# Changing the seam between two layers of a fused decoder step: the last six output strips of the first block computed by token halves, with its norms, residual and the first key and value strips

## The reference

```
layer 0:  proj = rms_norm(x, g_pre0) @ a_w_in                  # 2048 -> 2 x 2560
          xr, gate = halves of proj;  xc = causal conv(xr), 4 taps
          h = gated linear recurrence over the tokens (RG-LRU)
          out = (h * silu(gate)) @ a_w_out                     # 2560 -> 2048
          x1 = x + rms_norm(out, g_post0)
shared:   s = rms_norm(x1, kv_norm);  k = s @ w_k;  v = s @ w_v   # 4 heads of 128
layer 1:  q, gate = rms_norm(x1, g_pre1) @ b_w_in              # 16 heads of 128
          o = stick_breaking_attention(q, k, v, paged cache);  out = (o * silu(gate)) @ b_w_out
          y = x1 + rms_norm(out, g_post1)
outputs:  y, the new k and v, the last conv inputs (3 rows) and the last h of every sequence
rms_norm(x, g) = x / sqrt(mean(x*x over the width) + 1e-6) * g
```

## Time and profile before

| | us |
|---|---|
| median of 3 runs | 1816.08 (1814.78 to 1818.33) |
| profiled execution, its own time | 1814.62 |
| its span in the trace | 1812.9 |
| PE busy | 1740.7 (96%) |
| PE weight loads busy | 1666.8 (92%) |
| DVE busy | 1041.8 (57%) |
| ACT busy | 846.8 (47%) |
| POOL busy | 232.2 (13%) |
| share of PE in the chain that ended last | 88% |

### The profile page before, as it was taken

The page is one execution under the profiler, slowest core; times in us unless marked ns, Lnnn a source line. Parts: engine busy times, 40 slices in busy tenths (PEclk is TensorE's granted clock), DMA queues, the critical chain, the costliest instruction groups (busy, mean ns, idle before and its releaser), DMA issues.

```text
span 1812.9 us, 35653 instructions
## 1 busy us (share of the span) xinstructions
PE 1740.7 (96%) x14127; PEld 1666.8 (92%) x14127; DVE 1041.8 (57%) x1725; ACT 846.8 (47%) x1310; POOL 232.2 (13%) x175
## 2 busy tenths in 40 slices
PE   6999999999999999996999999999999999999997
PEld 5999999999999999995899999999998888799995
DVE  4766556666557522227757566565665666632365
ACT  4444443344444322223366666665675555722343
POOL 2000000000000000102132222322421111001110
PEclk9999999999999999998999999999999999999997
DMA  8322323322322223325432222222224777623565
GB/s 250 109 84 80 92 81 91 94 83 79 92 81 70 82 87 87 87 87 165 134 94 59 67 74 70 72 71 59 83 59 133 216 231 217 183 71 92 140 182 178
DMA packets 293525, 197.98 MB, mean 109 GB/s; under 512 B 8379, under 2 KB 267579, under 8 KB 293307
## 3 DMA queue, kind: packets, MB, share of 16 engines
q1 hardware_dynamic: 290632, 187.36, 35.4%
q0 software_dynamic: 2720, 8.78, 1.3%
q10 hardware_dynamic: 68, 0.41, 0.1%
HBM read 180.55 MB, written 15.97 MB: 108 GB/s over the span
## 4 chain that ended last, share of the span: by engine, by line
PE 88%; DVE 7%; issue 2%; ACT 1%; DMA 1%; SPq 0%; POOL 0%; ACTq 0%; DVEq 0%
PE PS L727 25%; PE PS L729 24%; PE PS L728 24%; PE Z L996 2%; PE Z L1006 1%; PE Z L727 1%; PE Z L729 1%; PE Z L728 1%; DVE T L1960 1%; DMA xin<-in_x_prompt_dram 1%; DVE WS L1672 1%; PE Z L1030 1%; PE Z L1189 1%; PE Z L905 1%; PE Z L936 1%
## 5 line engine op out<-in xcount | busy, mean ns | idle before, releaser
L727 PE MATMUL PS<-U,WS 128*128 128x272 f32 x3680 | 1075.7, 292 | 26.8 <-DVE U L1937 14.6
L729 PE MATMUL PS<-U,WS 128*128 128x272 f32 x3680 | 1065.2, 289 | 0.0
L728 PE MATMUL PS<-U,WS 128*128 128x272 f32 x3680 | 1062.6, 289 | 0.0
L727 PEld LDWEIGHTS PS<-U,WS 128*128 128x128 f32 x3680 | 694.5, 189 | 40.9 <-issue 25.1
L728 PEld LDWEIGHTS PS<-U,WS 128*128 128x128 f32 x3680 | 694.2, 189 | 0.9
L729 PEld LDWEIGHTS PS<-U,WS 128*128 128x128 f32 x3680 | 693.7, 188 | 0.0
L1672 DVE TENSOR_TENSOR WS<-raw,WS 128x1024 fp32r<-128x1024 f32 (+1 forms) x223 | 278.5, 1249 | 372.9 <-ACT WS L1221 369.9
L1221 ACT ACTIVATE WS<-raw 128x1024 fp32r<-128x1024 f32 (+1 forms) x225 | 231.1, 1027 | 531.2 <-PE PS L729 529.4
L640 POOL TENSOR_TENSOR raw<-raw,GN 128x1024 f32<-128x1024 f32 x80 | 157.9, 1974 | 556.3 <-DMA raw<-in_b_w_in_dram 470.5
L649 POOL COPY T<-T 128x544 f32<-128x544 f32 x2 | 1.7, 866 | 609.2 <-ACT T L1360 560.9
L652 POOL TENSOR_TENSOR T<-T 128x544 f32<-128x544 f32 x24 | 34.2, 1427 | 280.4 <-ACT T L1360 280.4
(11 more groups left out here) (288 smaller groups left out, 2042.2 us busy)
## 6 DMA issues: line engine op xcount, KB each, us to landing
raw<-in_a_w_in_dram SPq DMA_DIRECT2D x80, 512.0 KB, 3.8
raw<-in_b_w_in_dram SPq DMA_DIRECT2D x64, 512.0 KB, 4.1
raw<-in_a_w_out_dram SPq DMA_DIRECT2D x32, 512.0 KB, 3.9
KPG<-in_cache_k_dram SPq DMA_DIRECT2D x64, 256.0 KB, 3.2
raw<-in_b_w_out_dram SPq DMA_DIRECT2D x32, 512.0 KB, 4.0
VPG<-in_cache_v_dram SPq DMA_DIRECT2D x60, 256.0 KB, 3.0
RAW<-in_b_w_out_dram SPq DMA_DIRECT2D x12, 512.0 KB, 4.5
scratch_x<-T POOLq DMA_DIRECT2D x16, 272.0 KB, 3.6
```

The costliest lines, as they stand in the source:

```text
L727: pe.matmul(psum, w_hi, x_hi, start=first, stop=False)
L728: pe.matmul(psum, w_hi, x_lo, start=False, stop=False)
L729: return pe.matmul(psum, w_lo, x_hi, start=False, stop=last)
```

## The change

The last six strips of B are computed by token halves, in the way of E's last six: first the six strips for tokens 0 to 271 (units v = 0 to 17), then for tokens 272 to 543 (v = 18 to 35). A half strip is 20 tiles x 3 = 60 matmuls, in units of 8, 8 and 4 tiles. The first norm is done for each half by itself (3 columns of sums, the root on 128 x 3 values, then spread by a diagonal matrix). While PE works on the units from v = 21 on, the residual of the first half is done, one tile behind each unit, with its high part, square and rest; PE adds its squares from unit 23 on. The units of the first k and v strips are loaded as units 36 to 39 of the same ring, and both strips run for the first half and then, tile by tile, for the second. ACT takes them out of PSUM unscaled; DVE scales them after the second norm. The turns of k and v go to D's unit 6. The state rows are turned within B's second pair, one group behind each unit, and POOL stores them.

```diff
-D0 = B0 + 3 * KD
+B_FULL, B_SPLIT = KD - 6, 6
+BH0 = B0 + 3 * B_FULL
+BH_UNITS = 6 * B_SPLIT
+X1_AT = 3 * B_SPLIT + 3
+D0 = BH0 + BH_UNITS
+RING2 = (BH_UNITS + 4) // 4
...
-TURN_AT = {4: 0, **{FIRST_STEP - 1 + 2 * HEAD_STRIPS * k: k for k in range(1, NKV)}}
+TURN_AT = {FIRST_STEP - 1 + 2 * HEAD_STRIPS * k: k for k in range(NKV)}
...
+            def load_half_b(v):
+                if v < 2:
+                    sp.wait_ge(w_low, BH0 + v - 1)
+                elif v < 4:
+                    sp.wait_ge(state_out, 64)
                 else:
-                    col = (k * GRP + g) * DH + (D if kind == "gate" else 0)
-                    src = w_in_b[:, u * UT:(u + 1) * UT, col:col + DH]
-                load_unit(D0 + n, u, src)
-            for n in range(2):
-                load_d(n)
+                    sp.wait_ge(w_low, BH0 + v - 3)
+                if v < BH_UNITS:
+                    o, u = b_strip(v)[1], v % 3
+                    from_ = w_out_a[:, u * UT:u * UT + B_TILES[u], o * P:(o + 1) * P]
+                else:
+                    from_ = d_weights(v - BH_UNITS)
+                sp.dma_start(half_raw(v)[:, 0:b_tiles(v)], from_).then_inc((unit_in, b_half_in)[v // 2 % 2][v % 2], 16)
             sp.wait_ge(y_done, KR)
             for o in range(4):
-                reload(xT, False, o)
-            for n in range(2, 4):
+                for h in range(2):
+                    reload(h, o)
+            for v in range(BH_UNITS + 4):
+                load_half_b(v)
+                for o in range(4, KD):
+                    if min(X1_AT + o + 3, BH_UNITS + 3) == v:
+                        reload(0, o)
...
-                sp.wait_ge(x1_sum, o + 1)
+                sp.wait_ge(x1_sum[0], o + 1)
+                sp.wait_ge(x1_sum[1], o + 1)
                 sp.dma_start(x1T[o], Y[:, o, :]).then_inc(x1_kept, 16)
                 if o + 4 < KD:
-                    reload(xT, False, o + 4)
-            sp.wait_ge(st_out, 5)
-            conv_p, h_p, conv_s, h_s = out[2], out[3], out[6], out[7]
-            sp.dma_start(conv_p[0, 0], srow[ST_CP:ST_CP + SW, :]).then_inc(stored, 16)
-            sp.dma_start(h_p[0], srow[ST_HP:ST_HP + 1, :]).then_inc(stored, 16)
-            sp.dma_start(conv_s.rearrange("b l w n -> (b l w) n"), srow[ST_CS:ST_CS + NB * SW, :]).then_inc(stored, 16)
-            sp.dma_start(h_s.rearrange("b l n -> (b l) n"), srow[ST_HS:SCOLS, :]).then_inc(stored, 16)
+                    reload(1, o + 4)
...
+            for hs in range(2 * B_SPLIT - 1):
+                add_half_square(hs)
+            for n in range(3):
+                fold_first(n)
+            add_half_square(2 * B_SPLIT - 1)
+            fold_first(3)
...
+            def turn_states(n):
+                pe.wait_ge(gates_out, 4 * NBLK)
+                pe.wait_ge(y_done, KR)
                 if n >= 2:
                     pe.wait_ge(st_out, n - 1)
                 for t in range(4):
                     ins = pe.transpose(Z[0:SCOLS, 1, n % 2, t * P:(t + 1) * P], SO[:, 4 * n + t, :], IDN[:])
                 ins.then_inc(st_t, 1)
...
+            pair_b(1, lambda n: turn_states(n) if n < 5 else None)
...
+            def first_sums(h):
+                if h == 0:
+                    pe.wait_ge(st_out, 5)
+                pe.wait_ge(sq_sum, B_FULL + B_SPLIT * (h + 1))
+                for t, c in enumerate(HALF_COLS):
+                    ins = pe.matmul(Z[:, 1, 0, t:t + 1], T[:, 6, h * HALF + c:h * HALF + c + P], ONE[:, 0:1],
+                                    start=True, stop=True)
+                ins.then_inc(ms_done, 1)
+            def first_spread(h):
+                pe.wait_ge(diag_ready, 2 + h)
+                pe.matmul(Z[:, 1, 1, 0:HALF], ONE[:], T[:, 7, half(h)], start=True, stop=True).then_inc(ms_done, 1)
+            def square_sum(h, o):
+                pe.wait_ge(x1_sq[h], o + 1)
+                pe.matmul(Z[:, 0, h, 0:HALF], ONE[:], T[:, 4 + o % 2, half(h)], start=o == 0, stop=o == KD - 1,
+                          skip_group_check=True).then_inc(x1_squares[h], 1)
...
+            for v in range(BH_UNITS):
+                half_unit_b(v)
+                if v == 3 * B_SPLIT:
+                    first_sums(0)
+                if v == 3 * B_SPLIT + 1:
+                    first_spread(0)
+                if v >= X1_AT + 2:
+                    square_sum(0, v - X1_AT - 2)
+            def first_head(h, kt, s):
+                parts = half_parts(BH_UNITS + 2 * s + kt // UT)
+                c = kt % UT
+                pe.wait_ge(x1_low[h], kt + 1)
+                return three_pass(PS[:, s, h, 0:HALF], parts[:, 0, c, :], parts[:, 1, c, :], U[:, x_hi(kt), half(h)],
+                                  U[:, x_lo(kt), half(h)], kt == 0, kt == KD - 1)
+            pe.wait_ge(w_low, D0 + 1)
+            for kt in range(UT):
+                first_head(0, kt, 0)
+            square_sum(0, BH_UNITS - X1_AT - 2)
+            first_sums(1)
+            pe.wait_ge(w_low, D0 + 3)
+            for kt in range(UT):
+                first_head(0, kt, 1)
+            first_spread(1)
+            pe.wait_ge(w_low, D0 + 4)
+            for kt in range(UT, KD):
+                for s in range(2):
+                    ins = first_head(0, kt, s)
+                    if kt == KD - 1:
+                        ins.then_inc(kv_half, 1)
+                if kt > BH_UNITS - X1_AT - 2:
+                    square_sum(0, kt)
+            for kt in range(KD):
+                for s in range(2):
+                    if kt == 0:
+                        pe.wait_ge(strip_out, SD0 - 1 + s)
+                    ins = first_head(1, kt, s)
+                    if kt % UT == UT - 1:
+                        ins.then_inc(unit_done, 1)
+                if kt:
+                    square_sum(1, kt - 1)
+            square_sum(1, KD - 1)
...
+            def half_high_b(v):
+                if v < 2:
+                    act.wait_ge(unit_done, BH0 + v - 1)
+                elif v >= 4:
+                    act.wait_ge(unit_done, BH0 + v - 3)
+                if v >= BH_UNITS:
+                    act.wait_ge(w_fold, v - BH_UNITS + 1)
+                elif v // 2 % 2:
+                    act.wait_ge(b_half_in[v % 2], 16 * (v // 4 + 1))
+                else:
+                    act.wait_ge(unit_in[v % 2], 16 * (BH0 // 2 + v // 4 + 1))
+                nc.scalar.activation(half_parts(v)[:, 0, 0:b_tiles(v)], half_raw(v)[:, 0:b_tiles(v)], ACT.Copy).then_inc(w_high, 1)
...
+            def x1_split(h, o):
+                act.wait_ge(x1_sum[h], o + 1)
+                nc.scalar.activation(U[:, o, half(h)], Y[:, o, half(h)], ACT.Copy).then_inc(x1_high[h], 1)
+                if o >= 2:
+                    act.wait_ge(x1_squares[h], o - 1)
+                elif o == 0:
+                    act.wait_ge(sq_sum, B_FULL + B_SPLIT * (h + 1))
+                nc.scalar.activation(T[:, 4 + o % 2, half(h)], Y[:, o, half(h)], ACT.Square).then_inc(x1_sq[h], 1)
+            half_high_b(1)
+            for v in range(BH_UNITS):
+                half_high_b(v + 2)
+                if v and v % 3 == 0:
+                    half_square_b(v // 3 - 1)
+                if v == 3 * B_SPLIT + 1:
+                    first_root(0)
+                if v >= X1_AT:
+                    x1_split(0, v - X1_AT)
+            half_high_b(BH_UNITS + 2)
+            half_square_b(2 * B_SPLIT - 1)
+            for o in range(BH_UNITS - X1_AT, KD):
+                x1_split(0, o)
+            first_root(1)
+            half_high_b(BH_UNITS + 3)
             for o in range(KD):
-                act.wait_ge(x1_sum, o + 1)
-                nc.scalar.activation(U[:, o, :], Y[:, o, :], ACT.Copy).then_inc(x1_high, 1)
-                square(KD + o, o % 2, Y[:, o, :])
-                if o == UT + 2:
-                    high(D0 + 2, 0, 0, folded=True)
-            root(2)
+                x1_split(1, o)
+                if o == UT + 3:
+                    for which in range(2):
+                        act.wait_ge(kv_half, which + 1)
+                        act.wait_ge(ms_done, 2 + which)
+                        nc.scalar.activation(T[:, 6 + which, half(0)], PS[:, which, 0, 0:HALF], ACT.Copy)
+                    high(D0 + 4, 0, 0, done=D0 + 1, folded=True)
+            for which in range(2):
+                act.wait_ge(unit_done, D0 + 3 + which)
+                act.wait_ge(ms_done, 4 + which)
+                nc.scalar.activation(T[:, 6 + which, half(1)], PS[:, which, 1, 0:HALF], ACT.Copy).then_inc(strip_out, 1)
+            high(D0 + 5, 1, 0, done=D0 + 3, folded=True)
+            root2()
...
+            def first_norm(h):
+                hms, hy, hr, ht = (RT[:, n, 0:3] for n in range(4))
+                dve.wait_ge(ms_done, 2 + 2 * h)
+                V.tensor_scalar(hms, Z[:, 1, 0, 0:3], 1.0 / D, EPS, ALU.mult, ALU.add).then_inc(ms_out, 1)
+                dve.wait_ge(ms_root, 2 + h)
+                steps.done(V.reciprocal(hr, hy))
```

(74 more changed lines are left out.)

243 lines of the change are left out of this document (142 added, 101 removed).

## The result

The changed kernel takes 1821.56 us (median of 15 runs) where the kernel before takes 1817.21 in the same comparison: ratio 1.0023, 95% interval 1.0016 to 1.0030. It is slower by 0.23%, or 4.3 us. The forecast was 5.1 us slower, at 1821.2.

What follows compares the result with a forecast made beforehand. PE was taken as full except in one hole, where 25.2 us could be won; the new order's losses summed to 30.3, so 5.1 us longer, 1821.2 us, range 1811 to 1828.

Steps and rivals of the forecast that it cites:

- Transposes: The 20 state transposes, moved between units of B's second pair: the same 2.4 us of PE, nothing to add.
- Start of the halves: Turn from full to half strips in B: PE loses 1.3 us (0.5 to 2), as at E's identical turn.
- Tail and folds: First half, units 21 to 35: ACT and DVE alternate, +5.9 us; POOL folding gain into units 36 to 39, +2.8.
- Norm of the second half: First k tile to second half's norm: a chain of 10.5 us where PE has 3.5 of work, +7.0 (3 to 9).
- Behind the small sums: After PE's sums for the second half's norm: fourth fold holds DVE, +2.2 us; 8 tiles at lower clock, +1.3.
- Second half of k and v: Tiles wait for ACT's square and copy order, +3.1 us; extra ACT and DVE work at tile 11, +2.9.
- Second norm: D's unit 6 waits for the second norm's operations, 12.8 us or so against 12.1 of cover: +2.6 (0.5 to 5).
- Clock: Between B's last unit and the second norm PE falls to 1.2 GHz once more: +1.3 us (0 to 3).
- Rival 1: POOL and DVE do not hold each other up in this stretch: 7.3 us of lock terms go, 1814; chance 0.22.
- Rival 2: Units 21 to 35: ACT and DVE keep ahead of PE, step 3.0 us or less; 13 us faster, 1803; chance 0.13.
- rival 3: Second half: x tiles late (0.3 us on each of 12) and lower clock lasting (2 us); 1826; chance 0.15.
- Rival 4: The edits work as said and PE's clock never falls: 1.3 us less, inside the forecast's range; no chance of its own.

## Why the prediction was right, and where it was not

The forecast holds in sign, in size (5.1 against 4.3) and in mechanism. I set its steps against the time that TensorE lost in the trace after: from start to start, less its work at the forecast's 0.126 us a matmul and 0.45 a sum of squares. (Such a loss is up to 0.4 us more than the bracket shows, since the bracket begins where the profile ends the matmul ahead.)

- Transposes: 2.4 said, 2.1 measured. Start of the halves: 1.3 said, a wait of 1.23.
- Tail and folds: 5.9 + 2.8 = 8.7 said, 8.0 lost, before units 30, 31 and 33 and the first k tile. The step was right (11.03 against 11.2 for three), and the lead too: unit 24 was split 4.6 us after unit 21 began, 4.7 said. Four times the 0.17 is most of the difference.
- Norm of the second half: 7.0 said, 6.6 lost. The chain from the first k tile to the small sums was reckoned at 10.5 and took 10.03, of which 3.5 are work. The wait reads only 4.89 because the 8 k tiles ran at the lower clock and took 4.5 us (850.33 to 854.85) in place of 3.0; with the clock held up the chain took the same 10.03.
- Behind the small sums: 2.2 for the fourth fold and 1.3 for the clock said, 3.6 lost up to 868.03. The 8 v tiles took 5.5 us there (861.66 to 867.19) in place of 3.0, which looks like the clock's doing; but with a clock of 0.89 the same stretch took 7.83 in place of 7.67, so the 3.6 belong to the chain over VectorE.
- Second half of k and v: 3.1 + 2.9 said, 7.0 lost up to unit 4, with tiles of 1.40 and a wait of 2.99; changing ScalarE's order there gave 6.7 to 7.3.
- Second norm: 2.6 said, 2.2 lost, 1.86 of it as the wait.
- Clock: one fall said, three seen. The first two cost nothing, because the chains of the norm ran beside them. The third came after a wait of only 2.99 us, cost 1.9, and is the reason why the second half lost, and its new order gave, more than my 6.0.
- Rival 1 (no lock) is out: VectorE's operations of 1.77, 2.15 and 2.04 stand beside folds. Rival 2 needed a step of 3.0 us; it was 3.68. Of rival 3 one half came, a lower clock in the second half, but no late x tile that TensorE waited for. Rival 4 is out, since the clock fell.

With the 1.2 of norm work these losses come to about 30 us, where the sum had 30.3. No step is off by more than 1.0, but the net of 5.1 is small beside the two sums it is taken from, and that it came out within 1 us is also luck: the errors of -0.7, -0.4, +0.1, +1.0 and -0.4 nearly cancel. The 24.7 us that the sum's closing sentence gives to the old hole do not follow from it (it has 25.2); nothing rests on them.

The ledger had one weakness. It treats tail, folds, norm and clock as terms side by side, and the tail's 5.9 gave 10.7 when it was removed: 7.2 before the first k tile and 3.5 between it and the small sums, whose wait fell from 4.89 to 2.81. The 7.0 of the norm was in part the tail's lateness a second time. The sum was right, the shares weren't; someone who had read the list as a list of what each repair brings would have ranked the tail beside the norm, and it was worth more.

## What to carry to other kernels

When a stage is interleaved into the matmuls that hid nothing before, write down for each step which engine waits for which, and let each engine do first what the other's current work doesn't need: two such reorderings (the tail's on VectorE, the second half's on ScalarE), with no operation added, turned 0.23% slower into 0.7% faster. An ordering fault is priced together with all that stands behind it, so repair the earliest one first and measure again. A lower clock of the busiest engine costs only where that engine is not about to wait for another anyway (nothing at the first two falls, 1.9 us at the third). Work that stood in a hole of the busiest engine is not free once it is moved out of it (the transposes, 2.1 us).
